# One DMA store issued between two groups of weight loads instead of behind them, in the up stage of an MLP

## The reference

```python
h = layer_norm(ALPHA * x + mix, ln1_g, ln1_b)
f = jnp.einsum('btf,fd->btd', jnp.square(jax.nn.relu(jnp.einsum('btd,df->btf', h, w_mlp1))), w_mlp2)
y = layer_norm(ALPHA * h + f, ln2_g, ln2_b)
```

## Time and profile before

| | us |
|---|---|
| median of 3 runs | 2790.84 |
| lowest and highest | 2786.51, 2794.95 |
| profiled execution, its time | 2794.95 |
| profiled execution, its span in the trace | 2793.1 |

### The profile page before, as it was taken

How to read it: one execution, slowest core, us unless ns; L and a number is a source line. 1 busy time by engine, 2 the same in 40 slices (tenths; PEclk the granted TensorE clock), 3 DMA queues, 4 the chain that set the end, 5 groups by cost and what they waited for, 6 DMA issues and landing times.

```text
span 2793.1 us, 52028 instructions
## 1 busy us (share of the span) xinstructions
PE 2618.1 (94%) x20033; PEld 2487.4 (89%) x20033; DVE 1955.2 (70%) x3064; ACT 1047.5 (38%) x1311; POOL 51.9 (2%) x106
## 2 busy tenths in 40 slices
PE   8999999997888779995999999999989999999996
PEld 8999999994555559984999999999889999999995
DVE  4777722336763343349888888888868888888897
ACT  3111111116763441125555555555423333333334
POOL 0000000000001000000000000000000000000000
PEclk9999999998999889997999999999999999999998
DMA  8776543215025444322555555555685556565532
GB/s 249 231 240 215 166 80 86 76 45 218 0 92 195 183 145 144 122 73 98 180 192 180 179 182 192 199 188 192 222 308 189 185 177 209 185 186 185 180 114 71
DMA packets 470707, 457.36 MB, mean 164 GB/s; under 512 B 47740, under 2 KB 418644, under 8 KB 459830
## 3 DMA queue, kind: packets, MB, share of 16 engines
q1 hardware_dynamic: 465370, 389.02, 44.0%
q0 software_dynamic: 4608, 67.11, 6.4%
q10 hardware_dynamic: 652, 0.18, 0.0%
HBM read 367.70 MB, written 96.80 MB: 166 GB/s over the span
## 4 chain that ended last, share of the span: by engine, by line
PE 64%; DVE 5%; DMA 3%; issue 2%; ACT 1%; SPq 1%; DVEq 0%; POOL 0%; POOLq 0%; ACTq 0%
PE ps L2235 48%; PE ps L1899 7%; DMA sg<-in_cache_slc,idx 3%; PE ps L2041 1%; PE ps L2152 1%; PE ps L2051 1%; PE ps L2117 1%; PE ps L2104 1%; DVE pS L1385 1%; PE ps L2130 1%; PE ps L2065 1%; SPq L526 1%; DVE y_t L1617 0%; DVE h_t L1617 0%; ACT pS L834 0%
## 5 line engine op out<-in xcount | busy, mean ns | idle before, releaser
L934 ACT ACTIVATE w_sh<-w_s 128x1024 fp32r<-128x1024 f32 (+1 forms) x512 | 473.3, 948 | 815.6 <-PE ps L2235 527.2
L2235 PE MATMUL ps<-h_b,w_sh 128*128 128x288 f32 x3584 | 717.4, 296 | 29.6 <-DVE h_b L1642 21.6
L2235 PE MATMUL ps<-f_b,w_sh 128*128 128x288 f32 x3584 | 717.6, 296 | 17.1 <-DMA f_b<-f_scratch 11.2
L1537 DVE TENSOR_TENSOR w_sl<-w_s,w_sh 128x1024 fp32r<-128x1024 f32 (+1 forms) x512 | 554.2, 1088 | 125.5 <-ACT w_sh L934 125.2
L2235 PEld LDWEIGHTS ps<-h_b,w_sh 128*128 128x128 f32 x3584 | 578.0, 190 | 31.5 <-DVE h_b L1642 14.9
L2235 PEld LDWEIGHTS ps<-f_b,w_sh 128*128 128x128 f32 x3584 | 577.2, 189 | 20.1 <-DMA f_b<-f_scratch 12.1
L2235 PE MATMUL ps<-h_b,w_sl 128*128 128x288 f32 x1792 | 529.0, 295 | 0.0
L2235 PE MATMUL ps<-f_b,w_sl 128*128 128x288 f32 x1792 | 528.6, 295 | 0.0
L738 ACT ACTIVATE w_hi<-w_raw 128x2048 fp32r<-128x2048 f32 x61 | 117.0, 1918 | 618.6 <-PE ps L1899 614.0
L2235 PEld LDWEIGHTS ps<-h_b,w_sl 128*128 128x128 f32 x1792 | 340.9, 190 | 0.0
L2235 PEld LDWEIGHTS ps<-f_b,w_sl 128*128 128x128 f32 x1792 | 340.6, 190 | 0.0
(11 more groups left out here) (272 smaller groups left out, 2627.8 us busy)
## 6 DMA issues: line engine op xcount, KB each, us to landing
w_s<-in_w_mlp SPq DMA_DIRECT2D x512, 256.0 KB, 3.8
f_scratch<-f_st SPq DMA_DIRECT2D x32, 2016.0 KB, 8.9
f_b<-f_scratch SPq DMA_DIRECT2D x56, 1152.0 KB, 8.3
w_raw<-in_w_in SPq DMA_DIRECT2D x90, 512.0 KB, 5.2
x_r<-x_scratch SPq DMA_DIRECT2D x16, 576.0 KB, 5.2
wb<-in_cache_win SPq DMA_DIRECT2D x8, 1024.0 KB, 9.9
w_raw<-in_w_out SPq DMA_DIRECT2D x64, 128.0 KB, 2.9
w_raw<-in_w_out SPq DMA_DIRECT2D x16, 512.0 KB, 4.2
```

The costliest lines, as they stand in the source:

```text
L934: nc.scalar.activation(w_sh[m][:, :, :], blocks, ACT.Copy).then_inc(z_h[m], 1)
L1537: nc.vector.tensor_tensor(w_sl[m][:, :, :], blocks, w_sh[m][:, :, :].bitcast(F32), ALU.subtract).then_inc(z_l[m], 1)
L2235: last = nc.tensor.matmul(ps[:, bank, 0:TH], w[b][:, at_, cols], acts(k, x), start=(start and k == 0 and n == 0), stop=(stop and k == CK - ...
```

## The change

In SyncE's loop over i, `f_store(i)` stood behind both groups of loads. Now it stands between them: behind the loads into raw buffer 0 and ahead of the loads into raw buffer 1. No instruction is added or removed, and the other four engines have the same program as before.

```diff
             with sp.Fori(0, KP - 2) as i:
                 up_load(i + 2, 0)
+                f_store(i)
                 up_load(i + 2, 1)
-                f_store(i)
```

## The result

| | before | changed |
|---|---|---|
| median | 2792.56 us (4 runs) | 2889.11 us (4 runs) |
| lowest and highest | 2786.51, 2794.95 | 2884.69, 2892.32 |
| profiled execution | 2794.95 (span 2793.1) | 2880.25 (span 2878.5) |

The changed kernel is slower: the ratio is 1.034, 95% interval 1.0315 to 1.0368, or 96 us between the medians. The prediction said 51 us (2842) with a range to 2874. The direction and the chain of causes came out as forecast, the size did not.

A forecast was written before the change was run, and what follows sets the result against it. TensorE was taken to bound the up stage, with no wait to remove. Transfers 9.85 + VectorE 14.15 = 24.0 us an iteration, 1.79 longer; over 30 iterations, less cushions, 51 us on the 2790.84 median: 2842 us, range 2808 to 2874.

The forecast's parts named there:

- TensorE has nothing to give and the loads are just in time: Up stage: TensorE busy 22.20 of 22.20 us; blocks land about 0.1 us before VectorE's `sum_1` wants them.
- not slower: Rival: DMA engines take the loads' packets alongside the store's, so loads land in time; 2791 us, chance 0.10.
- SyncE's issues: SyncE in the loop: store issued at 1606.5 instead of 1609.34, loads into buffer 1 issued when they are now.
- signs of being wrong: Landing time under 5.6 us, VectorE waiting but iteration still 22.2 us, or the loads' issue delayed on SyncE.
- The store's passage: DMA engines, store ahead of loads: 0.5 us to start moving, 4.8 us for 2.06 MB at some 430 GB/s.
- The loads' own time: Four loads into buffer 1 behind the store: 4.4 us, between 3.2 and 5.4, the last landing at 1616.2.
- VectorE's part of the ring: From `sum_1` to the next `f_low`'s end: 14.95 us now, less 0.8 us of vanishing waits and early starts, 14.15.
- the ring: Up-stage cycle: `f_low` ends, store and loads run, `sum_1` starts, VectorE works to next `f_low`'s end; 24.0 us, 22.21 now.
- The sum over the loop: 30 iterations: `sum_1` late by 2.6 + 29 x 1.79 = 54.5 us; less 0.8 and a 2.8 cushion, TensorE 51 late.
- the long pair: Rival: store holds DMA engines longer than its rate says, pair takes its present 11.1 us; +93 us, 2884, chance 0.15.
- the price of a transfer: Skill's 2.0 us plus bytes at 436 GB/s: 9.1 us for 3.11 MB, loads landed at 1615.6, +33 us.
- the third rival: TensorE's waits lower its clock, 1.7 us each; once an iteration hides in 24.0, twice gives about +99 us, 2890; chance 0.05.

The follow-up runs named there:

- e5: Changed kernel with SyncE waiting for VectorE's add between the store and the loads into raw buffer 1, so these join 2.5 us later: 2878 us (one run).
- e1: Changed kernel with SyncE waiting until the store has landed before issuing the loads into raw buffer 1: 2916 us (one run).
- e7: Changed kernel with VectorE's `f_low` one instruction earlier, ahead of `sum_23`: 2861 us, ratio 1.0233.
- e3: Changed kernel with the store issued by ScalarE on its own queue, SyncE keeping only the loads: 2886 us, ratio 1.0322.

## Why the prediction was wrong in size, point by point

**TensorE has nothing to give and the loads are just in time.** Right. No rival of "not slower" had a chance: VectorE waited 29 times for the loads, 4.0 us at the longest.

**SyncE's issues.** Right for the store, 0.17 us behind `f_low`, and for the first load, 0.77 us behind it. What I did not foresee is that issuing behind the store is slow. The four loads into buffer 1 in the changed kernel:

```profile
1638.97 3.62 SPq L526 DMA_DIRECT2D w_s<-in_w_mlp  x3
...
1642.77 1.20 SPq L526 DMA_DIRECT2D w_s<-in_w_mlp  x1
```

They take 5.0 us in all, where they took 2.04. That the loads' issue is delayed was one of my signs of being wrong; it costs nothing here, since the loads wait for the store anyway, and e5 delays the issues further with no loss. It makes the fourth load's landing time a poor sign: I said about 7.5 us, it is 6.7, counted from its late issue:

```profile
w_s<-in_w_mlp SPq DMA_DIRECT2D x1, 256.0 KB, 6.7
```

**The store's passage.** This is the step that failed: "1606.5 + 0.5 + 4.8 gives 1611.8 for the DMA engines to be free". That is 5.3 us after the store's issue. Alone the store is through after 5.9 (e1), and with the loads queued behind it, its end being slow, after 7.2; it lands 1.4 us later (e1, e5). The slow end is the term that I did not have, and it has the size of the gap: 9.85 + 1.4 = 11.25 against 11.33 measured. In the kernel before, the loop's next loads came when the store was nearly through the earlier trace rows, so its rate there could not show it.

The lone example of the earlier trace rows could. I read 11.7 - 6.8 = 4.9 us and found my 4.8 confirmed. But the 6.8 of the earlier trace rows is the median of two loads, of which the second stands behind the first. Taken one at a time, in the trace of the kernel before, first the load issued at 2004.35 and then the one behind it:

```profile
f_b<-f_scratch SPq DMA_DIRECT2D x1, 1152.0 KB, 5.5
```

```profile
f_b<-f_scratch SPq DMA_DIRECT2D x1, 1152.0 KB, 8.1
```

With nothing ahead of it the load takes 5.5 us. Being behind the store cost 11.7 - 5.5 = 6.2 us, not 4.9, and the 7.4 us of that store to its landing, against 6.2 for one alone, was the slow end itself: its seventh and eighth packets took 0.85 and 1.25 us where alone they take 0.6 (stretches from 2060.10 to 2060.40, share 2.82, and from 2060.85 to 2061.40, share 2.27). I had put this down as a rival of 0.15.

**The loads' own time**, 4.4 us as the middle of 3.2 and 5.4, was 0.5 us too long: from the store's end, 7.2 us after its issue, to `sum_1`, 11.2 us after it, it is 3.9 to 4.0 us. The store's start and passage without the slow end, 0.5 + 4.8, were 0.6 us too short. That the sum with 1.4 us more comes out within 0.1 us is owed to these two errors, which cancel.

**VectorE's part of the ring**, predicted at 14.15 us, is 14.0 us; e7 confirms that this ring is what counts. TensorE waits for the low parts of M1, as forecast, but longer than the 1.1 and 0.7 us, and not always twice: 45 waits in 29 iterations, 2.5 us at the longest. Its weight loads in the changed kernel:

```profile
1653.63 0.30 PEld L2235 LDWEIGHTS ps<-h_b,w_sh 128*128 128x128 f32 x2 [1.52 <-DVE w_sl L1537]
...
1665.33 0.30 PEld L2235 LDWEIGHTS ps<-h_b,w_sh 128*128 128x128 f32 x2 [0.56 <-DVE w_sl L1537]
...
1678.95 0.30 PEld L2235 LDWEIGHTS ps<-h_b,w_sh 128*128 128x128 f32 x2 [2.44 <-DVE w_sl L1537]
```

**The sum over the loop.** With 11.33 + 14.0, the first late `sum_1` is 4.1 us late and each further one 3.12 us more. For the 29 iterations that wait: 4.1 + 28 x 3.12 - 3.6 = 88 us, against 90 us in the loop of the profiled execution and 96 between the medians. The rival "the long pair" had this size, 93 us and 2884. It named the right step, a store that holds the DMA engines longer than its rate says, but took its size from the pair in the other order, where the loads go first and the store has nothing behind it for most of its way; that the size fits is luck.

**Ring order and the price of a transfer.** The rule of the Trainium skill that descriptors start in ring order ("DMA: Bandwidth & Descriptors", "Queues, rings and completion order") fits the changed kernel, but e3 shows that another ring gives the loads no way past either. The price of 2.0 us plus bytes at 436 GB/s (same page, "Anatomy of one DMA") would have given +33 us. From the store's issue to `sum_1` it allows 9.1 us, where 11.2 are measured, so the measurement decides against it here; the slow end is 1.4 of these 2.1 us.

**The clock.** I said that it stays at 1.00. Three iterations in a row in the changed kernel, columns as in the earlier trace rows:

```profile
1613.02:1638.35 25.33, 22.78 (x158) 22.31 (x158) 19.62 (x26) 11.80 (x13) 0.00 (x0) 0.93 0.54 164
1638.35:1663.70 25.35, 24.06 (x182) 23.83 (x182) 19.65 (x26) 11.83 (x13) 0.00 (x0) 1.00 0.54 164
1663.70:1689.02 25.32, 22.79 (x170) 22.32 (x170) 19.63 (x26) 11.82 (x13) 0.00 (x0) 1.00 0.54 164
```

The first has a mean of 0.93, so a fall to the half level for part of it, and lasts 25.33 us like the others. TensorE's waits swallowed it: the wait at 1653.63, behind that turn, is 1.52 us, where the one at 1678.95, behind a turn at full clock, is 2.44. So the third rival came in part, and at no cost, as its own sum said for one fall an iteration. The Trainium skill ("TensorE: Matmul & The Clock Gate", section "HAM oscillation — how this bites in real kernels") tells of a loop in which a wait for data in every turn brings the half clock in every turn. That is not what happened here: two of these three turns kept the full clock.

## What to carry to other kernels

Where the engines' programs and the transfers form a ring (a buffer's last reader releases the load that its first reader waits for), a microsecond more for the transfer costs a microsecond in every iteration once the slack is gone, so look for the load that lands last before its reader, and put nothing large ahead of it. In sizing what stands ahead, take landing times one transfer at a time and note what is queued behind each; a median over two transfers in a line hides the very thing that is wanted. Moving the bulky transfer to another engine's queue did not help here (e3), where it had the earlier start.

## What the runs showed of the hardware

- A store of 2016 KB from SBUF to DRAM lands after 6.2 us with nothing behind it, after 6.9 with one load of 256 KB behind it, and after 7.6 with four. With a store of 864 KB behind one of 1152 KB there is no such loss (6.3 us for both). Whether it takes reads behind the store, or small pieces (512 bytes in the loads), and what in the chip does it, the runs do not show.
- The loss lies in the store's last two packets on each DMA engine: 1.0 and 1.3 us for 16128 bytes, where the packets take 0.6 us with nothing behind the store (e1).
- SyncE issues four loads behind the store in 5.0 us, where four with no store ahead took 2.04 us.
- A load issued on SyncE's queue 0.6 us after a large store on ScalarE's queue landed after 7.8 us, as late as in the same queue (8.0 us).
